# High weights against both parts of the activations in one product of 512 columns, in nine projection groups

## The reference, cut to what matters

```python
h = rms_norm(x, norm1_g)
z = h @ w_in                    # 2048 x 11272: fq, fk, fv, ff, hq, hf, hi, hgate, ga, gb
ya = forgetting_attention(fq, fk, fv, log_sigmoid(ff + bias)) @ w_a_up
ob = hgrn2_recurrence(silu(hq), 1 - f_gate(hf), hi, log(f_gate(hf)))   # then normed and gated
x = x + (sigmoid(ga) * ya + sigmoid(gb) * (ob @ w_b_up)) @ w_o
h2 = rms_norm(x, norm2_g)
q = h2 @ peer_wq                # 2048 x 2048, against the product keys of 8 heads
x = x + experts(h2, best 16 of 128 x 128 pairs of keys per head)       # U[ib], Vt[ib] gathered
return rms_norm(x, norm_f_g)
```

## Time and profile before

| | |
|---|---|
| three runs | 2051.21, 2050.98, 2048.92 us; median 2050.98 |
| the profiled execution | 2056.76 us; its span 2055.0 us, mean granted clock 0.841 |
| TensorE products | 1437.8 us busy (70%), 7933 |
| VectorE | 1609.0 us busy (78%) |
| ScalarE, GpSimd | 868.0 us (42%), 991.2 us (48%) |
| HBM read | 598.29 MB, 292 GB/s over the span |

### The profile page before, as it was taken

How to read it: one execution, slowest core, us unless ns; L and a number is a source line. 1 busy time by engine, 2 the same in 40 slices (tenths; PEclk the granted TensorE clock), 3 DMA queues, 4 the chain that set the end, 5 groups by cost and what they waited for, 6 DMA issues and landing times.

```text
span 2055.0 us, 22565 instructions
## 1 busy us (share of the span) xinstructions
PE 1437.8 (70%) x7933; PEld 1251.2 (61%) x7933; DVE 1609.0 (78%) x1995; ACT 868.0 (42%) x1130; POOL 991.2 (48%) x699
## 2 busy tenths in 40 slices
PE   6999999999999999920000001222348999999997
PEld 6987998877888789920000001111237888888886
DVE  5465775555745556789999999977988999999998
ACT  4353433344343444311111226567756444444444
POOL 1002320000000000178888888888888768888782
PEclk9999999999999999965555555555569999999999
DMA  5555434444555554789999999999955999999996
GB/s 206 185 185 184 163 124 144 154 144 164 184 184 190 199 185 164 266 352 411 421 422 412 415 402 410 414 421 412 421 220 186 390 386 390 393 406 393 394 388 229
DMA packets 151803, 601.81 MB, mean 293 GB/s; under 512 B 14720, under 2 KB 14736, under 8 KB 118288
## 3 DMA queue, kind: packets, MB, share of 16 engines
q0 software_dynamic: 58048, 364.41, 43.8%
q1 hardware_dynamic: 93648, 236.02, 32.1%
HBM read 598.29 MB, written 2.10 MB: 292 GB/s over the span
## 4 chain that ended last, share of the span: by engine, by line
PE 54%; DVE 17%; issue 13%; POOL 7%; DMA 6%; ACT 2%; SPq 0%; DVEq 0%; POOLq 0%; ACTq 0%
PE acc L1706 7%; PE acc L1708 7%; DVE slots L1461 7%; PE acc L1707 7%; POOL slots L536 5%; PE acc L1689 4%; PE acc L1691 4%; PE acc L1692 4%; DMA v_raw<-in_v_dense 3%; PE acc L2012 3%; PE scr L2013 3%; PE acc L2013 3%; PE scr L2012 3%; PE scr L2014 3%; PE acc L2014 3%
## 5 line engine op out<-in xcount | busy, mean ns | idle before, releaser
L942 DVE TENSOR_TENSOR w_lo<-raw,w_hi 128x2048 fp32r<-128x2048 f32 x136 | 314.7, 2315 | 284.5 <-ACT w_hi L597 283.4
L1461 DVE SCALAR_TENSOR_TENSOR slots<-slots,acc 128x2048 f32<-128x2048 f32 x188 | 424.6, 2285 | 46.0 <-DMA slots<-in_peer_u,expert 43.8
L597 ACT ACTIVATE w_hi<-raw 128x2048 fp32r<-128x2048 f32 x136 | 260.1, 1913 | 409.5 <-PE acc L1708 267.2
L581 POOL DMA_INDIRECT starts<-in_v_gather,expert x256 | 360.1, 1407 | 93.8 <-DVE X L1611 80.0
L536 POOL DMA_INDIRECT slots<-in_peer_u,expert x256 | 250.2, 977 | 244.7 <-DVE expert L1433 145.2
L544 POOL TENSOR_TENSOR slots<-slots,N 128x2048 f32<-128x2048 f32 x62 | 280.6, 4525 | 38.8 <-DMA slots<-in_peer_u,expert 38.6
L878 ACT ACTIVATE v_hi<-v_raw 128x1344 fp32r<-128x1344 f32 x128 | 170.5, 1332 | 264.1 <-PE scr L2014 194.3
L791 ACT ACTIVATE slots<-slots 128x2048 f32<-128x2048 f32 x62 | 118.4, 1910 | 342.3 <-POOL slots L544 342.3
L1969 PE MATMUL scr<-hot_a,hot_b 128*128 128x128 f32 x448 | 92.5, 372 | 222.2 <-DVE hot_b L1506 158.5
L1611 DVE SCALAR_TENSOR_TENSOR X<-starts,weight,X 128x704 f32<-128x704 f32 x256 | 242.2, 946 | 3.7 <-DMA starts<-in_v_gather,expert 3.4
L1706 PE MATMUL acc<-w_hi,hT_hi 128*128 128x512 f32 x576 | 227.6, 395 | 2.5 <-DVE w_lo L942 2.5
(11 more groups left out here) (297 smaller groups left out, 3113.8 us busy)
## 6 DMA issues: line engine op xcount, KB each, us to landing
raw<-in_w_in SPq DMA_DIRECT2D x88, 1024.0 KB, 4.9
v_raw<-in_v_dense SPq DMA_DIRECT2D x128, 672.0 KB, 7.5
raw<-in_w_o SPq DMA_DIRECT2D x16, 1024.0 KB, 5.1
raw<-in_peer_wq SPq DMA_DIRECT2D x16, 1024.0 KB, 5.1
raw<-in_w_a_up SPq DMA_DIRECT2D x8, 1024.0 KB, 5.1
raw<-in_w_b_up SPq DMA_DIRECT2D x8, 1024.0 KB, 5.0
slots<-in_peer_u,expert POOLq DMA_INDIRECT x256, 9.6
starts<-in_v_gather,expert POOLq DMA_INDIRECT x256, 8.1
```

What stands on the lines that cost most here:

```text
L581: pool.indirect_dma_start(starts[j][:, :], None, v_gather[:, :], bass.IndirectOffsetOnAxis(ap=expert[:, s // NSEL, s % NSEL:s % NSEL + 1], ...
L597: a.activation(w_hi[:, m % 2, :, :], raw[:, m % 2, :, :], ACT.Copy).then_inc(hi_ready, 1)
L942: v.tensor_tensor(w_lo[:, m % 2, :, :], raw[:, m % 2, :, :], w_hi[:, m % 2, :, :].bitcast(fp32), ALU.subtract).then_inc(lo_ready, 1)
L1461: v.scalar_tensor_tensor(out=slots[j][:, :], in0=slots[j][:, :], scalar=1.0, in1=row, op0=ALU.mult, op1=ALU.mult, accum_out=hid_sum[:, t, ...
```

## The change

In nine groups (1 to 3, 9 to 11, 35 to 37) the four units are cut otherwise. Before, a unit was 4 blocks `kk` and all 512 output columns. Now units 0 and 1 are the first 256 output columns with blocks 0 to 7 and 8 to 15, units 2 and 3 the other 256. The load of a unit thus takes 8 rows of 1 KB per partition instead of 4 of 2 KB (`load_pair_loop`). The high weights meet high and low activations in one product of 512 columns (`both[:, :, kk, :]`, two pieces of 256 columns, 16 KB apart in `hT_both` and 32 KB in `h2T_both`); the low weights meet the high activations in one of 256 as before. A unit is 16 + 16 products instead of 48. The 512 sums of an output block lie in one bank as two halves, and VectorE adds them as it copies out: `add_half`, a reduction from 1024 to 512 numbers per partition, once after unit 1 and once after unit 3, in place of the one `copy_group`. Each half of a group now takes one half of `acc` (`sums_of`, `sums_before` count their uses); TensorE waits for it at units 0 and 2. The first reductions of groups 1 to 3 come after `lo(g,3)`; in 9 to 11 after `lo(g,3)` and ahead of `place` and `times`; `query_half(n)` of 35 to 37 after `lo(g,3)`, for n > 1 with a wait for `score(n - 2)`, which read the same room. The second stand where the copies stood. The sums' places in groups 4 to 8 are swapped; nothing else is changed there.

```diff
+PAIRED = (*range(G_HQF + 1, G_HIG), *range(G_FQK + 1, G_FV), *range(G_WQ + 1, G_END))
+HALF = GW // 2
+def sums_of(g):
+    if g in PAIRED:
+        return (0, 1) if G_FQK < g < G_FV else (1, 0)
+    return ((g + (G_HIG <= g <= G_FQK)) % 2,)
+def sums_before(g, half, which):
+    uses = [which_of for other in range(g) for which_of in sums_of(other)] + list(sums_of(g)[:half])
+    return uses.count(which)
...
-        hT_hi = at("hT_hi", 16, [KD, S], f32r)
-        hT_lo = at("hT_lo", 32, [KD, S], f32r)
+        hT_both = at("hT_both", 16, [2, KD, S], f32r)
+        hT_hi, hT_lo = hT_both[:, 0, :, :], hT_both[:, 1, :, :]
...
+        h2T_both = at("h2T_both", 96, [3, KD, S], f32r)[:, 0:3:2, :, :]
...
+            def load_pair_loop(g0, groups, src, col0):
+                with sp.Fori(0, groups) as i:
+                    for m in range(4):
+                        sp.wait_ge(lo_ready, UNIT0[g0] + m + i * 4 - 1)
+                        sp.sem_inc(granted_w, 1)
+                        to = raw[:, m % 2, :, :].rearrange("p k n -> p (k n)").rearrange("p (k n) -> p k n", n=HALF)
+                        sp.dma_start(to, src[:, m % 2 * 2 * UK:(m % 2 + 1) * 2 * UK, ds(col0 + i * GW + m // 2 * HALF, HALF)]
+                                     ).then_inc(raw_landed[m % 2], 16)
...
-            load_loop(G_HQF + 1, 3, w_in_d, COL_HQ + GW)
+            load_pair_loop(G_HQF + 1, 3, w_in_d, COL_HQ + GW)
...
+            def add_half(g, half, to):
+                dve.wait_ge(unit_done, UNIT0[g] + 2 * half + 2)
+                which = sums_of(g)[half]
+                v.tensor_reduce(to[:, half * GW:(half + 1) * GW].rearrange("p (f s) -> p f s", f=2),
+                                acc[:, which, :].rearrange("p (f u s) -> p f s u", f=2, u=2),
+                                AX.X, ALU.add).then_inc(acc_free[which], 1)
...
+            def query_half(n):
+                if n > 1:
+                    dve.wait_ge(scr_ready[half_of(f"score{n - 2}")], use_number(f"score{n - 2}"))
+                add_half(G_WQ + n, 0, query_room(n))
             def copy_q(n):
-                copy_group(G_WQ + n, T2[:, D + n % 2 * 2 * GW:D + (n % 2 + 1) * 2 * GW])
+                if n:
+                    add_half(G_WQ + n, 1, query_room(n))
+                else:
+                    copy_group(G_WQ, query_room(0))
...
             lo(G_WQ + 1, 3)
+            query_half(1)
             select_part(0, 0, 3)
...
+            def paired_unit(g, m, both):
+                half = m // 2
+                which = sums_of(g)[half]
+                pe.wait_ge(lo_ready, UNIT0[g] + m + 1)
+                if m % 2 == 0:
+                    pe.wait_ge(acc_free[which], 1 + sums_before(g, half, which))
+                wh = w_hi[:, m % 2, :, :].rearrange("p k n -> p (k n)").rearrange("p (k n) -> p k n", n=HALF)
+                wl = w_lo[:, m % 2, :, :].rearrange("p k n -> p (k n)").rearrange("p (k n) -> p k n", n=HALF)
+                for k in range(2 * UK):
+                    kk = m % 2 * 2 * UK + k
+                    for f in range(2):
+                        cols = slice(f * P, (f + 1) * P)
+                        to = acc[:, which, f * GW:(f + 1) * GW]
+                        t_.matmul(to.rearrange("p (u s) -> p u s", u=2), wh[:, k, cols], both[:, :, kk, :],
+                                  start=kk == 0, stop=False, skip_group_check=True)
+                        last = t_.matmul(to[:, 0:S], wl[:, k, cols], both[:, 0, kk, :], start=False,
+                                         stop=kk == KD - 1, skip_group_check=True)
+                last.then_inc(unit_done, 1)
...
             for g in range(G_HQF + 1, G_HIG):
                 for m in range(4):
-                    transposed_unit(g, m, hT)
+                    paired_unit(g, m, hT_both)
```

More of the change, by code:

```diff
@@ L427, in _ @@
             sp.dma_start(ff_bias[:, :], fox_f_bias.rearrange("l h -> h l")).then_inc(small_in, 16)
-            load_loop(G_HQF + 1, 3, w_in_d, COL_HQ + GW)
+            load_pair_loop(G_HQF + 1, 3, w_in_d, COL_HQ + GW)
             load_loop(G_HIG, 4, w_in_d, COL_HI)
-            load_loop(G_FQK, 4, w_in_d, COL_FQ)
+            for m in range(4):
+                load(w_in_d, slice(COL_FQ, COL_FQ + GW), m, UNIT0[G_FQK] + m)
+            load_pair_loop(G_FQK + 1, 3, w_in_d, COL_FQ + GW)
             load_loop(G_FV, 2, w_in_d, COL_FV)
@@ L439, in _ @@
             load_loop(G_WO, 4, w_o_d, 0)
-            load_loop(G_WQ, 4, wq_d, 0)
+            for m in range(4):
+                load(wq_d, slice(0, GW), m, UNIT0[G_WQ] + m)
+            load_pair_loop(G_WQ + 1, 3, wq_d, GW)
             def load_v(n):
@@ L782, in rows_to_psum @@
                     if t == 0:
-                        act.wait_ge(acc_free[half], 1 + G_END // 2)
+                        act.wait_ge(acc_free[half], 1 + sums_before(G_END, 0, half))
                     a.activation(acc[:, half, :], N1[:, t, half * 2 * GW:(half + 1) * 2 * GW], ACT.Copy
@@ L1013, in copy_group, with hqf_half, fqk_half @@
                 dve.wait_ge(unit_done, UNIT0[g + 1])
-                src = acc[:, g % 2, :]
+                src = acc[:, sums_of(g)[0], :]
                 if len(to.shape) == 3:
                     src = src.rearrange("p (t n) -> p t n", t=NT)
-                v.tensor_copy(to, src).then_inc(acc_free[g % 2], 1)
-            def copied(g):
-                dve.wait_ge(acc_free[g % 2], g // 2 + 2)
-                dve.wait_ge(acc_free[1 - g % 2], (g + 1) // 2 + 1)
+                v.tensor_copy(to, src).then_inc(acc_free[sums_of(g)[0]], 1)
+            def add_half(g, half, to):
[4 more added lines that the diff above has]
+                                AX.X, ALU.add).then_inc(acc_free[which], 1)
+            def copied(g):
+                for which in range(2):
+                    dve.wait_ge(acc_free[which], 1 + sums_before(g + 1, 0, which))
+            def hqf_half(n, half):
+                add_half(G_HQF + n, half, Z1[:, n * 2 * GW:(n + 1) * 2 * GW])
+            def fqk_half(n, half):
+                add_half(G_FQK + n, half, Z2[:, n * 2 * GW:(n + 1) * 2 * GW])
             def hqf(n):
-                copy_group(G_HQF + n, Z1[:, n * 2 * GW:(n + 1) * 2 * GW])
+                if n:
+                    hqf_half(n, 1)
+                else:
+                    copy_group(G_HQF, Z1[:, 0:2 * GW])
             def hig(n):
@@ L1030, in fqk @@
             def fqk(n):
-                copy_group(G_FQK + n, Z2[:, n * 2 * GW:(n + 1) * 2 * GW])
+                if n:
+                    fqk_half(n, 1)
+                else:
+                    copy_group(G_FQK, Z2[:, 0:2 * GW])
             dve.wait_ge(wff_hi_ready, 1)
@@ L1765, in _ @@
                 for m in range(4):
-                    transposed_unit(g, m, hT)
+                    if n:
+                        paired_unit(g, m, hT_both)
+                    else:
+                        transposed_unit(g, m, hT)
                     if m % 2:
```

25 lines of the change are left out of this document (18 added, 7 removed).

## The result

Over 22 runs of each, the changed kernel took 2055.55 us (median; 2048.38 to 2059.48) and the kernel before 2050.45 (2046.77 to 2056.03): a ratio of 1.0020, 95% interval 1.0013 to 1.0028. It is slower, clear of noise: 4.2 us in the means, 5.1 in the medians, where the forecast was 2048.8, some 2.2 us faster. At 0.2% it lies on the edge of what the prediction calls slower, and 0.55 us above the upper end of the range. The profiled execution of the changed kernel took 2056.09 us with a span of 2054.4. That of the kernel before was 6 us above its own median, so the two traces differ by only 0.6 us, and single ends of the two can't be laid side by side. Stretches inside them can.

The account below looks back on a forecast made before the run. TensorE was taken to bound the projections (24 to 868 us), the DMA engines 884 to 1520 us. Products -5.2 plus last groups +3.0 made -2.2 us, 2048.8 from the median 2050.98; range 2043.5 to 2055.

Parts of the forecast that it names:

- 227 + 120 = 347: Paired units: a pair takes 347 ns instead of 360, 0.21 us a unit, 5.2 us over 25 units before score products.
- Not cheaper than two: Rival for the pairs: a product on two pieces takes 240 ns, nothing gained, last groups lose 3.6, 2054.6 us; chance 0.12.
- rule of the Trainium skill: Products: 262 cycles for 256 columns, 518 for 512, so an omitted product saves 2 to 3 ns, 25 units 1.0 us.
- late loads: Rival: 1 KB loads come too late in groups 1 to 3 and the last groups, +9.0 us, 2060.0; chance 0.07.
- slow reduction: Rival: VectorE's reduction takes 2.28 us across its step, +3.2 us on the forecast, 2052.0; chance 0.06.
- +3.0: Last three groups: 37.3 ends at 885.9 us, 3.0 after the 882.9 of the kernel before.
- I move that 1.6 to unit 37.1: Unit 37.1: after its wait the clock falls partly to 1.2 GHz, adding 1.6 us; it ends at 871.8.
- 1.08 + 1.22 = 2.3 us of idle: Before 36.0: TensorE's present wait of 1.08 us, with the next split ending 1.22 us later after group 35's added reduction.
- a second fall: Another fall of the clock makes the kernel slower; 0.02 of the forecast's 0.45 chance.
- The landing of 37.1: Load of 37.1 beside the gathers lands at 860.3 us, against 855.40 now; TensorE waits 5.6 us.
- packet by packet: Load of 37.1 beside gathers: queues alternate single packets, so 1 KB packets carry half, some 45 a us, 0.045 MB/us.
- 1.65 us alone: Load of 37.1 runs 1.65 us without gathers, moving 528 of its 1024 packets.

Follow-up runs that it names:

- side-by-side run: Changed kernel with the high and low part of each block of `hT` next to each other, so 512 columns are one piece; ratio 1.0027 to the kernel before.
- the last groups alone: Kernel before with only groups 35 to 37 in the new form; ratio 1.0028 to the kernel before.
- second profile: Kernel before run again with no edit; ratio 0.9992, 72.4 us from the start of score(0) to the last product of group 37.
- large loads: Changed kernel with groups 35 to 37 loading 2 KB pieces, as the kernel before does; ratio 1.0009 to the kernel before.
- the run with the split first: Changed kernel with VectorE's split of 36.0 moved ahead of the selection's part 4; ratio 1.0023 to the kernel before.
- small first sum: Changed kernel with the first reduction of group 35 summing 8 columns instead of 512; ratio 1.0004 to the kernel before.
- small loads alone: Kernel before with only the loads of 35 to 37 in 1 KB pieces, no pairs or reductions; ratio 1.0023 to the kernel before.
- the new order in the kernel before: Kernel before with split of 36.0 ahead of selection part 4, third and fourth gather behind 37.0 and 37.1; ratio 0.9997 to the kernel before.

## Why the prediction was wrong, by its own steps

**Products.** The step that failed is the sum "227 + 120 = 347": each duration was right by itself, but in alternation the pair took 353 in 17 of the 25 units ahead of score(0). By units that is 17 x 16 x 6.7 ns + 8 x 16 x 13 ns = 3.5 us, where 5.2 was forecast. The traces say the same: the five profiled kernels without early pairs start score(0) at 807.5 to 808.0 us, and three with them, and with the same falls of the clock ahead, at 804.2, 804.3 and 804.5: 3.4 us. In the changed kernel's own trace score(0) starts 6.4 us earlier (801.34 against 807.69), more than forecast; that is luck, since its clock rose earlier and fell once less on the way. The timed runs give 1.3, 1.3 and 2.9. "Not cheaper than two" at 240 was too much; its reason, the two pieces, is refuted by the side-by-side run. The rule of the Trainium skill that was weighed against the change ("TensorE: Matmul & The Clock Gate", Back-to-back issue gap) makes it 2 to 3 ns for each omitted product; by the trace it was 6.7 (360 less 353.3), and 13 in the eight units at 347.

**Sums and loads of groups 1 to 11.** Right in size and hidden, as foretold: no wait of ScalarE for a load before 115 us. The late loads and the slow reduction did not happen.

**The last groups.** The term "+3.0" was 5.7 in the trace, and 6.5 in the timed runs of the last groups alone. The position of the first wait was right to 0.1 us, and the time from the load's issue to ScalarE's start on it to 0.5. The step that failed is "I move that 1.6 to unit 37.1": it allowed one fall of the clock, of 3.4 us, behind the long wait. There were two. The one after 36.0 cost 1.3 us up to the score products. The prediction's own steps put 1.08 + 1.22 = 2.3 us of idle there, as much as the 2.24 ahead of the fall in the earlier trace rows, and still it left that clock at its higher level; a second fall was named only among the chances, at 0.02. The other lasted 6.8 us and cost 0.7 more. With 0.5 of landing that is 2.5 of the 2.7 us between forecast and trace. The trace of before is itself uncertain: against its second profile (72.4) the term would be 8.3.

**The landing of 37.1.** Right in size (13.3 us forecast from issue to landing, 13.8 measured to ScalarE's start) and right in its turns, packet by packet. The way there was in part wrong, so the size is in part luck: "1.65 us alone" was taken over from the kernel before. In fact the load's first packets came 3.5 us after its issue, behind two gathers, and it had its time alone only after the fourth. With large loads in the same order it still takes 13.0 us, so the forecast named one of two causes, each enough by itself. (Of the 54 writes of 4 bytes in the middle view of the earlier trace rows 16 are the load's and 38 the gathers', not 40 of the load's; it changes the turns little.)

**The sum.** -3.4 + 5.7 = +2.3 by the traces, and +2.7 to +5.7 by the interval. What stays open is some 2 us between these +2.3 and the +4.2 of the timed means. The early pairs show 3.4 us in the traces and 1.8 +- 0.5 over three timed comparisons. The traces of kernels with and without them also differ in when the clock first rises: at 18.1 to 19.3 us in six of the ten with early pairs, at 23.4 to 24.6 in the other four and in all five without. Most of those that rise early have one fall less between 380 and 510 us. No run isolates that.

## What to carry to other kernels

A product saved is worth its overhead only where TensorE is the bound and stays at the higher clock; two products over the columns of three saved 2% of a unit here. Beside a queue that already fills the engines, look first at what stands ahead of each load when it is issued, and beside it: putting two gathers off by 15 and 19 us gave the changed kernel 7.6 us, more than its products saved ahead of score(0). And price a new wait of TensorE of the size of these (2.7 and 5.7 us) twice, once for itself and once for the clock behind it.

## What was not expected of the hardware

- At the lower clock a product has no cost beyond its columns: 213 ns for 256 and 427 for 512, which is one column per cycle of 1.2 GHz, against 120 and 227 at the higher.
- The clock after a wait isn't a matter of its length alone. With waits of TensorE of 2.7 and 5.7 us went 3.4 and 6.8 us at the lower clock, with one of 7.9 us (the run with the split first) 10.2, but with those of 8.3 and 8.6 us (small first sum, small loads alone) 6.8. One of 2.5 us at 37.2 had 3.4 us, one of 2.4 us at 37.1 (the new order in the kernel before) none.
- A gather that begins 0.26 us after a split of VectorE takes 2.88 us to issue, one that begins 0.02 us after it 0.98. A quarter of a microsecond in the order of two queues decided whether 1 MB went ahead of a load or behind it.
- A load on another queue moved nothing for 3.5 us while gathers issued before it ran (1.1 us in the kernel before), though its packets then took turns with later ones.
- Between the two queues an engine changed after nearly every single packet, of 4 bytes, 1, 2 or 8 KB alike (358 of 373 steps).
